# Waits of TensorE for its own last tile around the feed-forward loops, and other start addresses for the rows it reads

## The chip, the cores and the metric

The kernel runs on one core of one Trainium2 chip. The metric is the time of one execution on the device in microseconds (us); lower is better. Before the change three runs gave 2365.05, 2376.81 and 2380.16 us; their median is 2376.81 us.

## What is computed

Two small transformer-like stacks, one after the other, on 256 tokens of width 1024 in fp32 (the first stack adds 16 meta tokens in front, so it works on 272 columns, and drops them at its end). Cut to what matters here:

```python
# first stack: 2 layers, 272 tokens
h = concatenate([meta, x], axis=1)
for l in range(2):
    h = h + 0.5 * swiglu(rms_norm(h, ffn1_norm[l]), ffn1_w_gu[l], ffn1_w_down[l])
    u = rms_norm(h, mix_norm[l])
    c_q, c_kv, k_pe, hq, hf, hi, hg, ga, gb = split_cols(u @ w_in[l], IN_SPLITS)
    y_a = mla(...) @ w_proj_attn[l]          # latent attention
    y_b = hgrn2(...) @ w_proj_rec[l]         # gated recurrence
    h = h + (sigmoid(ga) * y_a + sigmoid(gb) * y_b) @ w_out[l]
    h = h + 0.5 * swiglu(rms_norm(h, ffn2_norm[l]), ffn2_w_gu[l], ffn2_w_down[l])
x = rms_norm(h, final_norm)[:, 16:]
# second stack: 2 layers, 256 tokens: macaron_ffn, mixer, macaron_ffn in each
#   swiglu_2(x, ...) = (silu(x @ w_gate) * (x @ w_up)) @ w_down, width 1024 -> 2816 -> 1024
#   mixer of layer 0: causal convolution and a linear recurrence; of layer 1: attention
```

There are eight feed-forwards (FFNs) of the same size in all: four in the first stack and four in the second. Since the meta columns are dropped at the end, the last FFN of the first stack already works on 256 columns only.

## The kernel before

**Numbers.** Activations lie in SBUF with the feature on the partition and the token on the column. Every fp32 matrix product is made of three matmuls of a 128x128 weight block: weights and inputs are both split into a high and a low part (`whi`, `wlo`; `x_..._hi`, `x_..._lo`), and TensorE adds wlo*xhi + whi*xlo + whi*xhi (`split_product`, L607, L608, L609; the same three in `first_tiles`, L667 to L669). The moving operand of each is one row of an input tile: 272 columns in the first stack, 256 in the second and in those parts of the first stack's last stages that no longer need the meta tokens.

**Weights.** SyncE streams weight chunks from HBM into a ring of four slots (`raw`). ScalarE rounds a chunk to `whi` (L1000), VectorE makes `wlo` as the difference (L1399) and counts it in the semaphore `lo_made`. TensorE waits for it before each output tile, and counts each finished tile in `tile_done`.

**An FFN** (`ffn` in the TensorE program): 44 output tiles of gate and up (24 matmuls each, numbered 0 to 43), then 8 output tiles of down (66 matmuls each). Tiles 0 to 7 are written out in code; tiles 8 to 43 are one hardware loop (`pe.Fori`, L711) of nine rounds of four tiles; down is another loop (L729) of four rounds of two tiles (in the second stack three rounds, the last one is written out). Among the early tiles TensorE also makes the column sums for the norm and broadcasts the result (`norm_back_drained`: the broadcast matmuls at L625, and then a wait for the semaphore of the last of them, `back_made`). F6, the FFN behind the keys and values, leaves that out, since its norm exists already.

**Addresses.** The input tiles of all stages share one place. Their bases are multiples of 256 bytes plus a shift: `SHIFT` = 64 for the stages `0` (first FFN of a layer, `x_first`), `1` (mixer, `x_mixer`) and all 256-column stages (`x_tokens`), `BACK_SHIFT` = 192 for stage `2` (`x_second`, the second FFN of layer 0). A row of the 272-column tiles is 320 columns, 1280 bytes long, so every row has the shift of its tile. The hidden tiles (`hid_first`, `hid_second`, `hid_tokens`) are laid out alike. `cut(t, k, c)` picks row k from column c on: c is 0, or 16 where the meta tokens are left out. In the mixer of layer 1 there are 19 tiles with c = 0 and 20 with c = 16, out of `x_mixer`: the latter start at 64 + 16*4 = 128 bytes from a multiple of 256. The tile `mid` (input of the mixer's last eight tiles) has rows of 1088 bytes from a multiple of 256, so its rows begin at 0, 64, 128 and 192 in turn.

**What sets the order.** Everything is written out by hand: each engine has its own program, and the semaphores tie them. The TensorE loop that is touched:

```python
with pe.Fori(2, FFN_GU_QUADS) as b:
    for k in range(RING):
        k8_tile(b + q, k, b * RING + j + k - 3, k, X[s], c)
```

`k8_tile` waits for `lo_made` (L654) and for the bank to be read (`tile_read`, L656), and then makes the 24 matmuls.

Of the kernel before, what the change touches and what calls it, by code (L numbers as in the profile page):

```python
# [19 lines left out]
T = SEQ + N_META  # L20
# [23 lines left out]
RING = 4  # L44
# [216 lines left out]
def program(nc, a):  # L261
    with ExitStack() as ctx:
# [17 lines left out]
        LINE, SHIFT, BACK_SHIFT, ROW = 256, 64, 192, T + 48  # L280
# [6 lines left out]
        def line_after(place):  # L287
# [4 lines left out]
        X = {0: pair_at("x_first", KD, xbase + SHIFT, ROW), 1: pair_at("x_mixer", KD, xbase + SHIFT, ROW),  # L292
             2: pair_at("x_second", KD, xbase + BACK_SHIFT, ROW), "last": x_tokens, "F4": x_tokens, "REC": x_tokens,
             "F5": x_tokens, "F6": x_tokens, "ATT": x_tokens, "F7": x_tokens}
        top[0] = xbase + BACK_SHIFT + 2 * KD * ROW * 4
# [22 lines left out]
        HID = {0: pair_at("hid_first", KF, hbase + SHIFT, ROW), 2: pair_at("hid_second", KF, hbase + BACK_SHIFT, ROW),  # L318
               "last": hid_tokens, "F4": hid_tokens, "F5": hid_tokens,
               "F6": hid_tokens, "F7": hid_tokens}  # L320
        hid_end, ebase = hbase + BACK_SHIFT + 2 * KF * ROW * 4, hbase + BACK_SHIFT + 2 * KF * SEQ * 4
# [150 lines left out]
        def layer_stage(l, which):  # L472
            q, j, n = ((0, 0, 0), (FFN_QUADS, FFN_TILES, 1), (FFN_QUADS + MIX_QUADS, FFN_TILES + MIX_TILES, 2))[which]
            return dict(q=l * LAYER_QUADS + q, j=l * LAYER_TILES + j, x=l * 3 + which, n=l * 3 + n,
                        f=l * 2 + which // 2, c=N_META if (l, which) == (DEPTH - 1, 2) else 0, layer=True, s="last" if (l, which) == (DEPTH - 1, 2) else which)
# [40 lines left out]
        AFTER = {0: 1, 2: 0, "last": "F4"}  # L516
# [82 lines left out]
        def _(pe):  # L599
# [86 lines left out]
            def inputs_ready(x):  # L686
                return lambda i: pe.wait_ge(x_lo_made, x * 8 + i + 1)
# [14 lines left out]
            def ffn(q, j, x, n, f, c, layer, s, main_norm=True):  # L702
# [8 lines left out]
                with pe.Fori(2, FFN_GU_QUADS) as b:  # L711
                    for k in range(RING):
                        k8_tile(b + q, k, b * RING + j + k - 3, k, X[s], c)
# [14 lines left out]

                with pe.Fori(0, FFN_DOWN_QUADS if layer else FFN_DOWN_QUADS - 1) as b:  # L729
                    down(b)  # L730
# [3 lines left out]
            def mixer(l):  # L734
# [4 lines left out]
                for step, i in MIXER:  # L739
                    if (step, i) == ("tile", 0):  # L740
                        first_tiles(q, 2, X[1], 0, inputs_ready(x), input_norm(x, n, 0))
                    elif step == "tile" and i > 1:
# [3 lines left out]
                        hi, lo, at_k = sources.get(TILE[t][0], (*X[1], 0))  # L746
# [1411 lines left out]
```

## Time and profile before

| | |
|---|---|
| median of 3 runs | 2376.81 us |
| the profiled execution's own time | 2368.04 us |
| its span, first to last instruction | 2366.3 us |
| TensorE matmuls, busy | 2246.4 us, 95% |
| TensorE weight loads | 2206.1 us, 93% |
| VectorE / ScalarE / GpSimd | 59% / 49% / 23% |
| mean granted TensorE clock | 0.976 |

How to read it: "busy" of TensorE is time in which at least one matmul is in the array. Matmuls overlap, so a row's "mean ns of one" is longer than the distance between two starts (here called the pitch), and in a stretch without a gap the pitch is the length of the stretch over the number of matmuls that start in it. A count of a window also takes in the two or so that only reach into it.

### The profile page before, as it was taken

What the parts mean: (1) busy time and instruction counts of PE and PEld (TensorE: products, weight loads), DVE (VectorE), ACT (ScalarE), POOL (GpSimd) and SP (SyncE); (2) the same over time, 40 slices, a digit from 0 to 9 for tenths busy, and PEclk for the clock granted to TensorE, in tenths of its full rate; (3) what the DMA queues carried; (4) which work ended last, traced back from release to release, by engine and by line L of the source; (5) the groups of instructions that cost most, each with busy time, mean ns of one, the idle gap of its engine ahead of it and who ended that gap; (6) DMA issues with size and microseconds to landing.
All of it is one profiled execution on the core that took longest, in us unless ns stands there. A gap on an engine that the chain in (4) does not pass through costs nothing.

```text
span 2366.3 us, 49110 instructions
## 1 busy us (share of the span) xinstructions
PE 2246.4 (95%) x18270; PEld 2206.1 (93%) x18270; DVE 1398.5 (59%) x1966; ACT 1161.2 (49%) x1752; POOL 555.6 (23%) x589
## 2 busy tenths in 40 slices
PE   7999999999999999999999999985999999978998
PEld 7999988999999999888999899985999999978998
DVE  6555866655555557756565555476664655465553
ACT  5444544454345436444454455466554545455553
POOL 4322000232213220001332242024431132111420
PEclk9999999999999999999999999997999999998999
DMA  6554423455546545233565466442565556532663
GB/s 210 186 188 154 149 90 117 141 170 171 184 142 195 187 157 166 87 98 117 161 199 192 141 197 200 156 161 89 179 211 169 195 179 199 176 114 87 200 203 116
DMA packets 99258, 380.47 MB, mean 161 GB/s; under 512 B 10911, under 2 KB 13087, under 8 KB 99016
## 3 DMA queue, kind: packets, MB, share of 16 engines
q1 hardware_dynamic: 99144, 378.91, 49.5%
q8 instruction: 76, 1.25, 0.2%
q14 instruction: 38, 0.31, 0.0%
HBM read 377.80 MB, written 3.16 MB: 161 GB/s over the span
## 4 chain that ended last, share of the span: by engine, by line
PE 86%; DVE 6%; ACT 3%; issue 2%; DVEq 1%; POOL 1%; DMA 0%; ACTq 0%; SPq 0%
PE bank L607 26%; PE bank L608 25%; PE bank L609 25%; ACT whi L1000 2%; PE bank L667 2%; DVE wlo L1399 2%; PE bank L668 2%; PE bank L669 2%; PE bank L884 1%; PE bank L625 1%; PE bank L794 1%; PE bank L873 0%; DVE cv L1735 0%; PE bank L863 0%; POOL outlo L2042 0%
## 5 line engine op out<-in xcount | busy, mean ns | idle before, releaser
L1399 DVE TENSOR_TENSOR wlo<-raw,whi 128x1024 fp32r<-128x1024 f32 (+1 forms) x660 | 869.6, 1329 | 528.2 <-ACT whi L1000 525.8
L1000 ACT ACTIVATE whi<-raw 128x1024 fp32r<-128x1024 f32 (+1 forms) x660 | 729.2, 1117 | 439.9 <-PE bank L609 401.9
L607 PE MATMUL bank<-x_tokens_hi,wlo 128*128 128x256 f32 x1784 | 498.7, 280 | 4.3 <-DVE z L1751 3.6
L608 PE MATMUL bank<-x_tokens_lo,whi 128*128 128x256 f32 x1784 | 497.1, 279 | 0.0
L609 PE MATMUL bank<-x_tokens_hi,whi 128*128 128x256 f32 x1784 | 497.1, 279 | 0.0
L607 PEld LDWEIGHTS bank<-x_tokens_hi,wlo 128*128 128x128 f32 x1784 | 338.9, 190 | 5.9 <-issue 3.8
L608 PEld LDWEIGHTS bank<-x_tokens_lo,whi 128*128 128x128 f32 x1784 | 336.3, 189 | 0.0
L609 PEld LDWEIGHTS bank<-x_tokens_hi,whi 128*128 128x128 f32 x1784 | 336.0, 188 | 0.0
L1980 POOL TENSOR_TENSOR z<-sil,z 128x256 f32<-128x256 f32 (+1 forms) x176 | 176.4, 1002 | 567.7 <-DVE z L1443 416.3
L609 PE MATMUL bank<-hid_tokens_hi,whi 128*128 128x256 f32 x880 | 244.7, 278 | 0.0
L607 PE MATMUL bank<-hid_tokens_hi,wlo 128*128 128x256 f32 x880 | 244.6, 278 | 0.0
L608 PE MATMUL bank<-hid_tokens_lo,whi 128*128 128x256 f32 x880 | 244.6, 278 | 0.0
L607 PE MATMUL bank<-x_first_hi,wlo 128*128 128x272 f32 x672 | 192.9, 287 | 0.1
L608 PE MATMUL bank<-x_first_lo,whi 128*128 128x272 f32 x672 | 192.5, 287 | 0.0
L609 PE MATMUL bank<-x_first_hi,whi 128*128 128x272 f32 x672 | 192.5, 287 | 0.0
L607 PE MATMUL bank<-x_mixer_hi,wlo 128*128 128x272 f32 (+1 forms) x592 | 177.4, 300 | 1.3 <-DVE sgb L1515 1.2
L608 PE MATMUL bank<-x_mixer_lo,whi 128*128 128x272 f32 (+1 forms) x592 | 172.7, 292 | 0.0
L609 PE MATMUL bank<-x_mixer_hi,whi 128*128 128x272 f32 (+1 forms) x592 | 172.4, 291 | 0.0
L607 PEld LDWEIGHTS bank<-hid_tokens_hi,wlo 128*128 128x128 f32 x880 | 166.7, 189 | 0.0
L608 PEld LDWEIGHTS bank<-hid_tokens_lo,whi 128*128 128x128 f32 x880 | 165.2, 188 | 0.0
L609 PEld LDWEIGHTS bank<-hid_tokens_hi,whi 128*128 128x128 f32 x880 | 165.2, 188 | 0.0
L607 PEld LDWEIGHTS bank<-x_first_hi,wlo 128*128 128x128 f32 x672 | 126.6, 188 | 0.5 <-PE bank L625 0.5
(378 smaller groups left out, 4958.7 us busy)
## 6 DMA issues: line engine op xcount, KB each, us to landing
raw<-ffn_gu SPq DMA_DIRECT2D x352, 512.0 KB, 3.7
raw<-ffn_down SPq DMA_DIRECT2D x128, 704.0 KB, 4.1
raw<-mix SPq DMA_DIRECT2D x120, 512.0 KB, 3.5
raw<-rec SPq DMA_DIRECT2D x28, 512.0 KB, 3.9
raw<-kv SPq DMA_DIRECT2D x16, 512.0 KB, 4.4
raw<-att SPq DMA_DIRECT2D x16, 512.0 KB, 3.9
bias_rows<-rows SPq DMA_DIRECT2D x8, 256.0 KB, 4.3
bias<-bias_rows SPq DMA_DIRECT2D x1, 1536.0 KB, 9.0
```

What stands on the lines that cost most here:

```text
L607: pe.matmul(out, wlo[:, slot, w], xh(i), start=(i == 0), stop=False)
L608: pe.matmul(out, whi[:, slot, w], xl(i), start=False, stop=False)
L609: mm = pe.matmul(out, whi[:, slot, w], xh(i), start=False, stop=(i == last))
L625: mm = pe.matmul(out[:, at_t + t:at_t + t + P], inv[:, at_col + i:at_col + i + 1].to_broadcast([P, P]), ident, start=True, stop=True)
L667: pe.matmul(out, wlo[:, k, w], cut(hi, i, c), start=(i == 0), stop=False)
L668: pe.matmul(out, whi[:, k, w], cut(lo, i, c), start=False, stop=False)
L669: return pe.matmul(out, whi[:, k, w], cut(hi, i, c), start=False, stop=(i == 7))
L794: mm = pe.matmul(bank[NORM][:, 3 * col + s:3 * col + s + 1], src[:, at_t:at_t + P], ones[:, 0:1], start=(k == 0), stop=(k == len(parts) - 1))
L884: return pe.matmul(bank[b][0:size_s, col:col + size_t], keys[:, hd, s:s + size_s], qd[:, hd, t:t + size_t], start=True, stop=True)
L1000: act.activation(whi[:, k, 0:cols], raw[:, k, 0:cols], ACT.Copy).then_inc(hi_made, 1)
L1399: dve.tensor_tensor(wlo[:, k, 0:cols], raw[:, k, 0:cols], whi[:, k, 0:cols].bitcast(F32), ALU.subtract).then_inc(lo_made, 1)
L1980: pool.tensor_tensor(z[:, 2 + p, c:T], sil[:, p, c:T], z[:, 2 + p, c:T], ALU.mult).then_inc(hid_made, 1)
```

## The change

In `ffn`, TensorE's program: the loop over gate and up is cut in two (rounds 2 and 3, then 4 to 10), and ahead of each of the two loops and of the loop of down stands a wait for the finish of TensorE's own last tile (`tile_done`). That makes three waits in each of eight FFNs. In the layout: `BACK_SHIFT` is gone; `x_second` and `hid_second` start at 64; the stages of layer 1 have tiles with names of their own, of which `x_late` and `hid_late` lie as `x_first` and `hid_first` did, and `x_late_mixer` starts at 0, so that its column 16 starts at 64. What lies behind the two areas moves up by 64 bytes.

```diff
@@ -277,7 +277,7 @@
-        LINE, SHIFT, BACK_SHIFT, ROW = 256, 64, 192, T + 48
+        LINE, SHIFT, ROW = 256, 64, T + 48
@@ -289,10 +289,11 @@
-        X = {0: pair_at("x_first", KD, xbase + SHIFT, ROW), 1: pair_at("x_mixer", KD, xbase + SHIFT, ROW),
-             2: pair_at("x_second", KD, xbase + BACK_SHIFT, ROW), "last": x_tokens, "F4": x_tokens, "REC": x_tokens,
-             "F5": x_tokens, "F6": x_tokens, "ATT": x_tokens, "F7": x_tokens}
-        top[0] = xbase + BACK_SHIFT + 2 * KD * ROW * 4
+        X = dict.fromkeys(("last", "F4", "REC", "F5", "F6", "ATT", "F7"), x_tokens)
+        X.update({0: pair_at("x_first", KD, xbase + 64, ROW), 1: pair_at("x_mixer", KD, xbase + 64, ROW),
+                  2: pair_at("x_second", KD, xbase + 64, ROW), "late": pair_at("x_late", KD, xbase + 64, ROW),
+                  "late_mixer": pair_at("x_late_mixer", KD, xbase, ROW)})
+        top[0] = xbase + LINE + 2 * KD * ROW * 4
@@ -315,10 +316,10 @@
-        HID = {0: pair_at("hid_first", KF, hbase + SHIFT, ROW), 2: pair_at("hid_second", KF, hbase + BACK_SHIFT, ROW),
...
+        HID.update({0: pair_at("hid_first", KF, hbase + 64, ROW), 2: pair_at("hid_second", KF, hbase + 64, ROW),
+                    "late": pair_at("hid_late", KF, hbase + 64, ROW)})
+        hid_end, ebase = hbase + LINE + 2 * KF * ROW * 4, hbase + LINE + 2 * KF * SEQ * 4
@@ -472,7 +473,8 @@
-                        f=l * 2 + which // 2, c=N_META if (l, which) == (DEPTH - 1, 2) else 0, layer=True, s="last" if (l, which) == (DEPTH - 1, 2) else which)
+                        f=l * 2 + which // 2, c=N_META if (l, which) == (DEPTH - 1, 2) else 0, layer=True,
+                        s=which if l < DEPTH - 1 else ("late", "late_mixer", "last")[which])
@@ -513,7 +515,7 @@
-        AFTER = {0: 1, 2: 0, "last": "F4"}
+        AFTER = {0: 1, 2: "late", "late": "late_mixer", "last": "F4"}
@@ -708,9 +710,11 @@
-                with pe.Fori(2, FFN_GU_QUADS) as b:
-                    for k in range(RING):
-                        k8_tile(b + q, k, b * RING + j + k - 3, k, X[s], c)
+                for first, end in ((2, 4), (4, FFN_GU_QUADS)):
+                    pe.wait_ge(tile_done, first * RING + j)
+                    with pe.Fori(first, end) as b:
+                        for k in range(RING):
+                            k8_tile(b + q, k, b * RING + j + k - 3, k, X[s], c)
@@ -726,6 +730,7 @@
+                pe.wait_ge(tile_done, j + 2 * KF)
                 with pe.Fori(0, FFN_DOWN_QUADS if layer else FFN_DOWN_QUADS - 1) as b:
                     down(b)
@@ -738,12 +743,12 @@
-                        first_tiles(q, 2, X[1], 0, inputs_ready(x), input_norm(x, n, 0))
+                        first_tiles(q, 2, X[st["s"]], 0, inputs_ready(x), input_norm(x, n, 0))
...
-                        hi, lo, at_k = sources.get(TILE[t][0], (*X[1], 0))
+                        hi, lo, at_k = sources.get(TILE[t][0], (*X[st["s"]], 0))
```

TensorE's instructions where the loop over gate and up begins, in the first FFN, before: the last three matmuls of tile 7, the jump into the loop and the loop's first tile. `bank` is the PSUM bank written.

```order
L607 MATMUL bank<-x_first_hi,wlo 128x272
L608 MATMUL bank<-x_first_lo,whi 128x272
L609 MATMUL bank<-x_first_hi,whi 128x272
L711 UNCONDITIONAL_BRANCH
L711 ISA
L656 REGISTER_ALU [waits lo_made]
L607 MATMUL bank<-x_first_hi,wlo 128x272 [waits tile_read]
```

The same place with the change. The jump now waits for `tile_done`, and the register instructions that set up the loop stand behind it.

```order
L609 MATMUL bank<-x_first_hi,wlo 128x272
L610 MATMUL bank<-x_first_lo,whi 128x272
L611 MATMUL bank<-x_first_hi,whi 128x272
L715 UNCONDITIONAL_BRANCH [waits tile_done]
L715 ISA
L658 REGISTER_ALU [waits lo_made]
L609 MATMUL bank<-x_first_hi,wlo 128x272 [waits tile_read]
```

TensorE where tile 15 ends and tile 16 begins, in the first FFN with the change: before, both are rounds of one loop, and here a second loop is entered.

```order
L609 MATMUL bank<-x_first_hi,wlo 128x272
L610 MATMUL bank<-x_first_lo,whi 128x272
L611 MATMUL bank<-x_first_hi,whi 128x272
L715 REGISTER_ALU
L715 COMPARE_AND_BRANCH
L715 UNCONDITIONAL_BRANCH [waits tile_done]
L715 ISA
L658 REGISTER_ALU [waits lo_made]
L609 MATMUL bank<-x_first_hi,wlo 128x272 [waits tile_read]
```

Moved or added are these jumps with their waits and set-up, and the second copy of the loop's body; TensorE's written program grows from 8854 to 9709 such rows. No other engine's program gets an instruction more or less.

## Rows read from the trace of the kernel before

**Rows 1.** Page: span, busy us (share) xinstructions, and the chain that ended last.
```profile
span 2366.3 us, 49110 instructions
PE 2246.4 (95%) x18270; PEld 2206.1 (93%) x18270; DVE 1398.5 (59%) x1966; ACT 1161.2 (49%) x1752; POOL 555.6 (23%) x589
PE 86%; DVE 6%; ACT 3%; issue 2%; DVEq 1%; POOL 1%; DMA 0%; ACTq 0%; SPq 0%
```

**Rows 2.** Windows, TensorE: stretch, length, busy (x matmuls), granted clock, DMA share, GB/s.
```profile
50.00:140.00 90.00, 90.00 (x732) 1.00 0.58 190
160.00:210.00 50.00, 50.00 (x407) 1.00 0.48 157
515.00:605.00 90.00, 90.00 (x713) 1.00 0.58 184
625.00:675.00 50.00, 50.00 (x397) 1.00 0.44 147
1190.00:1260.00 70.00, 70.00 (x596) 1.00 0.62 200
1280.00:1330.00 50.00, 50.00 (x427) 1.00 0.49 158
1385.00:1455.00 70.00, 70.00 (x620) 1.00 0.66 208
1470.00:1520.00 50.00, 50.00 (x443) 1.00 0.52 171
1695.00:1765.00 70.00, 70.00 (x620) 1.00 0.67 210
1920.00:2000.00 80.00, 80.00 (x682) 1.00 0.65 197
2215.00:2285.00 70.00, 70.00 (x620) 1.00 0.68 208
```

**Rows 3.** Timeline, TensorE, tile 10 of the first stack's last FFN: start, length.
```profile
1175.29 0.28 PE L609 MATMUL bank<-x_tokens_hi,whi 128*128 128x256 f32 x1
1175.40 0.31 PE L607 MATMUL bank<-x_tokens_hi,wlo 128*128 128x256 f32 x1
1175.55 0.28 PE L608 MATMUL bank<-x_tokens_lo,whi 128*128 128x256 f32 x1
```

**Rows 4.** Timeline, VectorE, same place: the low part that tile 10 waits for.
```profile
1173.98 1.22 DVE L1399 TENSOR_TENSOR wlo<-raw,whi 128x1024 fp32r<-128x1024 f32 x1 [3.35 <-ACT whi L1000]
```

**Rows 5.** Timeline, TensorE: a wait for its own last matmul, in that FFN.
```profile
1163.68 0.67 PE L625 MATMUL bank<-consts,inv 128*128 128x128 f32 x4
1164.41 0.38 PE L607 MATMUL bank<-x_tokens_hi,wlo 128*128 128x256 f32 x1
1164.63 0.28 PE L608 MATMUL bank<-x_tokens_lo,whi 128*128 128x256 f32 x1
1164.74 0.28 PE L609 MATMUL bank<-x_tokens_hi,whi 128*128 128x256 f32 x1
```

**Rows 6.** TensorE's sequencer at the loops' starts: min/median/max ns, first and last start.
```profile
L711 PEldq MOVE  x1: 29/29/29, 1167.9 to 1167.9; - x1
L656 PEldq FUSED_REGOPS  x1: 43/43/43, 1168.1 to 1168.1; - x1
L729 PEldq MOVE  x1: 29/29/29, 1269.7 to 1269.7; - x1
L719 PEldq EVENT_SEMAPHORE  x1: 51/51/51, 1270.1 to 1270.1; - x1
```

**Rows 7.** Groups by form, 925:931 (mixer, c = 16), then 465:480 (tile mid).
```profile
L607 PE MATMUL bank<-x_mixer_hi,wlo 128*128 128x256 f32 x18 | 5.1, 283 | 0.0
...
L608 PE MATMUL bank<-midlo,whi 128*128 128x272 f32 x41 | 11.8, 288 | 0.0
L607 PE MATMUL bank<-midhi,wlo 128*128 128x272 f32 x40 | 11.6, 290 | 0.0
```

**Rows 8.** Groups by form, 1388:1400 (F4, gate and up); below 1183:1200 (last FFN).
```profile
L608 PE MATMUL bank<-x_tokens_lo,whi 128*128 128x256 f32 x36 | 9.9, 276 | 0.0
...
L609 PE MATMUL bank<-x_tokens_hi,whi 128*128 128x256 f32 x49 | 13.8, 281 | 0.0
```

**Rows 9.** Page, DMA queues: packets, MB, share of 16 engines over the span.
```profile
q8 instruction: 76, 1.25, 0.2%
```

More of the change, by code:

```diff
@@ L317, in program @@
         hid_tokens = pair_at("hid_tokens", KF, hbase + SHIFT, SEQ)
-        HID = {0: pair_at("hid_first", KF, hbase + SHIFT, ROW), 2: pair_at("hid_second", KF, hbase + BACK_SHIFT, ROW),
-               "last": hid_tokens, "F4": hid_tokens, "F5": hid_tokens,
-               "F6": hid_tokens, "F7": hid_tokens}
-        hid_end, ebase = hbase + BACK_SHIFT + 2 * KF * ROW * 4, hbase + BACK_SHIFT + 2 * KF * SEQ * 4
+        HID = dict.fromkeys(("last", "F4", "F5", "F6", "F7"), hid_tokens)
+        HID.update({0: pair_at("hid_first", KF, hbase + 64, ROW), 2: pair_at("hid_second", KF, hbase + 64, ROW),
+                    "late": pair_at("hid_late", KF, hbase + 64, ROW)})
+        hid_end, ebase = hbase + LINE + 2 * KF * ROW * 4, hbase + LINE + 2 * KF * SEQ * 4
         H, E = [hbase], [ebase]
```

## Prediction

> **What bounds the kernel.** I read the page's busy shares and its chain first: TensorE has a matmul in the array for 95% of the span and holds 86% of the chain that ended last [rows 1]. So nearly every nanosecond on the distance between two matmul starts (the pitch) is in the time, and little else is. Next I asked for windows in the middle of the FFNs' loops, where TensorE is busy throughout, and divided length by matmuls (less two that only reach into the window) [rows 2]. The order of those rows is: first FFN's gate/up and down, second FFN's gate/up and down, the last FFN's of the first stack gate/up and down, F4's gate/up and down, then gate/up of F5, F6 and F7. The pitches come out as follows.
> - 272 columns, rows at 64: 90/730 = 123.3 ns and 50/405 = 123.5 ns. Rows at 192 (second FFN of layer 0): 90/711 = 126.6 ns and 50/395 = 126.6 ns.
> - 256 columns, all at 64: F4 70/618 = 113.3 and 50/441 = 113.4 ns, F5 and F7 the same 113.3; but the last FFN of the first stack 70/594 = 117.8 and 50/425 = 117.6 ns, and F6 80/680 = 117.6 ns.
>
> The second line is the interesting one: one loop body, one layout, one granted clock (1.00), and two pitches. The timeline shows where the last FFN leaves the faster one: at tile 10 a matmul's successor comes 0.15 us later instead of 0.113, and behind it the steps are 0.12 [rows 3]. That tile waits for its low weights, which VectorE finishes at 1173.98 + 1.22 = 1175.20 us, after 3.35 us without work of its own [rows 4]; TensorE's queue had nearly run dry. I take it that how weight loads and matmuls interleave in the queue is a pattern that lasts until something disturbs it: a near-stall can leave the longer pitch, and a full stop brings the shorter one back, since after the stop at the norm's broadcast the pitch of that FFN is 0.11 us [rows 5], up to tile 10.
>
> **The waits, their gain.** If each loop starts from an empty array, the last FFN keeps 113.3 ns for tiles 10 to 43 and for down: 34*24*4.5 ns = 3.7 us and 8*66*4.3 ns = 2.3 us. F6, which has no such stop before, gains 36*24*4.3 ns = 3.7 us in its loop and, with the last FFN's price for down, 2.3 us. Together 12.0 us. At 272 columns I take nothing: pitch is 123.3 ns at 64 in all windows read, although those FFNs have the stop at the broadcast too, so no shorter pitch shows. F4, F5 and F7 have 113.3 ns already. The near-stall at tile 10 should not come back: the weights' chain runs on while TensorE stands 0.6 us at tile 8, so tile 10 is wanted 0.6 us later.
>
> **The waits, their cost.** There are 3*8 = 24. The nearest row is the stop at the broadcast: the four broadcast matmuls end at 1163.68 + 0.67 = 1164.35, so the last began at about 1164.07; two matmuls on is 1164.63, that is 0.56 us for two steps of 0.113: 0.33 us lost [rows 5]. Here more hangs behind the wait: the sequencer's set-up of the loop, which before ran ahead hidden by the queue. From the set-up's first instruction to its last before a matmul I read 1167.9 to 1168.1 us, some 0.25 us with the last one's length and the wake-up, for gate and up, and 1269.7 to 1270.1, some 0.45 us, for down [rows 6]. So 16*(0.33 + 0.25) + 8*(0.33 + 0.45) = 9.3 + 6.2 = 15.5 us. Lower bound: set-up hidden, 24*0.33 = 7.9 us. Upper bound: each start also pays one code chunk. The code queue moved 76 packets in 0.2% of 16 engines' span [rows 9], 0.002*16*2366/76 = 1.0 us each: 15.5 + 24 = 39.5 us. I take 15.5, since the taken jumps back in these loops leave no gap in windows that are busy throughout [rows 2]. Behind each wait only TensorE's own next tile is queued. VectorE and ScalarE get slack from it; the weight stream's slots come free 0.6 us later at a time, which nobody waits for while TensorE is the bound.
>
> The Trainium skill ("TensorE: Matmul & The Clock Gate", single matmul latency and back-to-back issue gap) gives (398+N)/2.4 ns for one warm matmul and N/2.4 + 2.5 ns between two, at N = 256 272.5 and 109.2 ns: a stop would cost 163 ns, an estimate from that page, and 24 of them 3.9 us; the trace's 0.33 us disagrees and decides.
>
> **Second FFN's rows at 64.** 44*24 matmuls at 126.6 - 123.3 = 3.3 ns: 3.5 us; 8*66 at 3.1 ns: 1.7 us. The two patterns do not blur this, as both FFNs have a stop at the broadcast and both keep their pitch. Gain 5.2 us; bounds 0 (the address isn't the cause) and 5.2.
>
> **Late mixer.** No row shows 272 columns from 0 alone. Tile `mid` has rows at 0, 64, 128, 192 in turn, and its matmuls take 288 to 290 ns [rows 7]. A matmul's length is its pitch and 163 ns more (276 at 113.3, 281 at 117.8) [rows 8, 2], so that is 126 ns on average, and rows at 0 and 128 would be at (4*126 - 123.3 - 126.6)/2 = 127.0 ns. The 19 tiles with c = 0 then lose 456*3.7 ns = 1.7 us (bounds 0 and 2.1). The 20 tiles with c = 16 go from 283 - 163 = 120 ns [rows 7] to 117.7 or 113.3, whichever pattern they are in: 480*2.3 = 1.1 or 480*6.7 = 3.2 us; I take the middle, 2.1. Net gain 0.4 us, between -1.0 and +3.2. The shift by 64 bytes of what lies behind the tiles is costed at nothing: those are operands of engines off the chain.
>
> **Sum.** Against the profiled execution's own 2368.0 us: -12.0 - 5.2 - 0.4 + 15.5 = -2.1, so 2366 us. That execution is 8.8 us below the runs' median. The runs span 15.1 us; if executions differ in how many FFNs run at 117.7 ns (6.0 us each), the median had one or two more than the profile, and the change would take those away too. I can't see that from one trace; I leave the forecast at 2366 and let the range reach up by most of those 8.8 us and more.
>
> **Rivals.**
> - *The short pitch is not kept* (0.12): another near-stall, or the new loop's first round, throws the FFNs back. For: F6 and the last FFN stayed at 117.7 ns for 100 us each. Against: F4, F5, F7 stay at 113.3 through their first round. Then the 12.0 us stay away: 2378 us.
> - *Slower, by code fetch behind the stops* (0.06): the program grows by 855 written rows, and an empty queue covers no fetch. At one chunk per stop 2366 + 24 = 2390 us; it decides for "slower" from (2400.6 - 2366)/24 = 1.4 us more per stop, 2 us in all, which is about two chunks (0.03). The Trainium skill ("Runtime: NRT & Kernel Launch", instruction fetch mechanics) says that a taken branch whose target isn't in the current two-page window forces a fetch before execution goes on; the loops' jumps back show no such gap here.
> - *The stops are cheap* (0.12): set-up hidden, 7.9 us, and the mixer's better end: 2368 - 12.0 - 5.2 - 3.2 + 7.9 = 2355.5 us, and further down only if other FFNs gain as well.
> - *Addresses do nothing* (0.05): 126.6 against 123.3 ns has another cause: 2366 + 5.6 = 2371.5 us. By the skill's gap formula, which knows no address, 272 columns take 115.8 ns anywhere; the rows at 64 and at 192 differ, so I trust it little here.
> - The forecast has the remaining 0.65.
>
> **Numbers.** A measurement of this kernel can tell about 1% from no change: 2353.0 to 2400.6 us. The forecast and three rivals lie inside; faster takes the far end of the cheap stops (0.05), slower two chunks at each stop (0.03), the rest 0.92. The range is 2354 to 2381: from the cheap stops to the short pitch not kept, with some of the runs' own spread.
>
> **What would show it.** TensorE's windows in the last FFN and F6 at 113.3 ns and in the second FFN at 123.3 ns show the gains right. Twenty-four new holes of 0.6 (gate/up) and 0.8 us (down) show the cost right; 0.33 or 1.6 us make the number wrong by 7 or 24 us. In the late mixer the matmuls with 272 columns should last 290 ns instead of 286, those with 256 between 276 and 281 instead of 283. A near-stall in rounds 2 and 3 that outlives the second stop would make the first term wrong.

## The result and the profile after

The changed kernel took 2388.95 us (median of 9 runs, 2383.79 to 2393.91) against 2372.30 us before (9 runs, 2365.05 to 2386.32): a ratio of 1.0065, 95% interval 1.0041 to 1.0088. It is slower by about 0.65%. That is inside the 1% called "the same" above, but it is a real loss, on the other side of the forecast's sign, and outside its range. The profiled execution took 2384.87 us, against 2368.04 before: 16.8 us more, which is what the medians differ by too.

The page of the changed kernel, against [rows 1] and [rows 9]. TensorE has the same 18270 matmuls, and is busy 5.8 us longer; the span is 16.8 us longer.

```profile
span 2383.1 us, 49118 instructions
PE 2252.2 (95%) x18270; PEld 2206.2 (93%) x18270; DVE 1402.8 (59%) x1966; ACT 1163.2 (49%) x1752; POOL 549.2 (23%) x589
q8 instruction: 82, 1.34, 0.2%
PE 82%; DVE 6%; ACT 5%; issue 3%; DVEq 2%; POOL 1%; POOLq 1%; DMA 0%; ACTq 0%; SPq 0%
```

Windows of TensorE in the changed kernel, 60 us in tiles 16 to 43 and 45 us in down, columns as in [rows 2]. In this order: second FFN of layer 0; last FFN; F4; F5; F6; F7.

```profile
541.00:601.00 60.00, 60.00 (x489) 1.00 0.59 176
625.00:670.00 45.00, 45.00 (x367) 1.00 0.47 155
1201.00:1261.00 60.00, 60.00 (x532) 1.00 0.64 201
1278.00:1323.00 45.00, 45.00 (x384) 1.00 0.49 161
1396.00:1456.00 60.00, 60.00 (x532) 1.00 0.64 202
1473.00:1518.00 45.00, 45.00 (x384) 1.00 0.48 162
1711.00:1771.00 60.00, 60.00 (x531) 1.00 0.64 203
1788.00:1833.00 45.00, 45.00 (x385) 1.00 0.48 159
1952.00:2012.00 60.00, 60.00 (x532) 1.00 0.63 198
2029.00:2074.00 45.00, 45.00 (x384) 1.00 0.49 164
2238.00:2298.00 60.00, 60.00 (x532) 1.00 0.64 201
2315.00:2360.00 45.00, 45.00 (x384) 1.00 0.42 136
```

Take two off each count, as in the prediction. The second FFN stands at 60/487 = 123.2 and 45/365 = 123.3 ns where it was 126.6: as forecast. Gate and up stand at 60/530 = 113.2 ns in all five FFNs with 256 columns: also as forecast. But down stands at 45/382 = 117.8 ns in **all five**, also in F4, which ran it at 113.4 before [rows 2].

The stop ahead of down in F4, from TensorE's timeline of the changed kernel (start, length, instruction): the last matmul of tile 43, then the first three of down.

```profile
1467.20 0.28 PE L611 MATMUL bank<-x_tokens_hi,whi 128*128 128x256 f32 x1
1468.03 0.35 PE L609 MATMUL bank<-hid_tokens_hi,wlo 128*128 128x256 f32 x1 [0.55 <-DVE wlo L1404]
1468.22 0.28 PE L610 MATMUL bank<-hid_tokens_lo,whi 128*128 128x256 f32 x1
1468.34 0.28 PE L611 MATMUL bank<-hid_tokens_hi,whi 128*128 128x256 f32 x1
```

And the first stop of F4, between tiles 7 and 8:

```profile
1368.03 0.28 PE L611 MATMUL bank<-x_tokens_hi,whi 128*128 128x256 f32 x1
1368.65 0.38 PE L609 MATMUL bank<-x_tokens_hi,wlo 128*128 128x256 f32 x1 [0.35 <-DVE z L1441]
1368.87 0.28 PE L610 MATMUL bank<-x_tokens_lo,whi 128*128 128x256 f32 x1
1368.99 0.28 PE L611 MATMUL bank<-x_tokens_hi,whi 128*128 128x256 f32 x1
```

The releasers named in brackets had long been done; what the wait is for is TensorE's own tile, and the profile puts it down to another semaphore. At down 0.83 us pass to the next start and then 0.19, for two steps of 0.113: 0.79 us lost. At the first stop it is 0.62 and 0.22, so 0.61 us lost. The forecast had 0.78 and 0.58.

The loops' entries, TensorE's sequencer: 16 set-ups for gate and up and 8 for down, where the profile of before has 8 and 8.

```profile
L715 PEldq MOVE  x16: 29/29/34, 44.8 to 2232.6; - x16
L734 PEldq MOVE  x8: 29/29/34, 152.5 to 2309.4; - x8
```

In the late mixer (groups by form, 928:934, then 898:922) the matmuls with 256 columns last 276 ns where they lasted 283 [rows 7], and those with 272 columns last 290, that is a pitch of 127.

```profile
L609 PE MATMUL bank<-x_late_mixer_hi,wlo 128*128 128x256 f32 x19 | 5.2, 276 | 0.0
...
L610 PE MATMUL bank<-x_late_mixer_lo,whi 128*128 128x272 f32 x64 | 18.5, 290 | 0.0
```

Two stretches outside the FFNs grew that no edit touches: the mixer's sums of layer 1, and the attention's scores and probabilities with the matmuls around them. The first window runs from the first matmul of the sums to the first broadcast matmul behind the tile that follows them; the second takes the same 112 matmuls in both kernels, the last two dozen of them already in the tiles behind the attention. Before:

```profile
1007.40:1019.40 12.00, 12.00 (x81) 0.72 0.17 53
2109.40:2147.00 37.60, 22.99 (x112) 0.86 0.09 29
```

After:

```profile
1009.87:1023.50 13.63, 13.63 (x81) 0.62 0.14 44
2117.80:2159.20 41.40, 27.61 (x113) 0.71 0.08 27
```

The mean granted clock was lower there: 0.62 against 0.72, and 0.71 against 0.86, so that more of the stretch ran at 1.2 GHz and less at 2.4.

### The profile page after: what moved, and what is told of

The parts are those of the page before. It is cut to its first block, busy times and chain, and to the rows that moved or that the text cites. A ratio compares the mean times of both kernels' runs of the same rounds, so it can differ in the third digit from the quotient of the medians.

```text
span 2383.1 us, 49118 instructions
## 1 busy us (share of the span) xinstructions
PE 2252.2 (95%) x18270; PEld 2206.2 (93%) x18270; DVE 1402.8 (59%) x1966; ACT 1163.2 (49%) x1752; POOL 549.2 (23%) x589
## 4 chain that ended last, share of the span: by engine, by line
PE 82%; DVE 6%; ACT 5%; issue 3%; DVEq 2%; POOL 1%; POOLq 1%; DMA 0%; ACTq 0%; SPq 0%
PE bank L609 24%; PE bank L610 24%; PE bank L611 24%; ACT whi L1005 3%; DVE wlo L1404 2%; PE bank L669 1%; PE bank L670 1%; PE bank L671 1%; PE bank L889 1%; PE bank L627 1%; PE bank L799 1%; POOLq L1965 1%; PE bank L878 0%; DVE cv L1740 0%; PE bank L868 0%
## 5 line engine op out<-in xcount | busy, mean ns | idle before, releaser
L1985 POOL TENSOR_TENSOR z<-sil,z 128x256 f32<-128x256 f32 (+1 forms) x176 | 167.1, 949 | 573.3 <-DVE z L1448 424.5
L1441 DVE TENSOR_TENSOR z<-bank,rstd 128x256 f32<-128x256 f32 (+1 forms) x176 | 75.4, 428 | 74.6 <-PE bank L611 61.4
L1989 POOL TENSOR_TENSOR hid_tokens_lo<-z,hid_tokens_hi 128x256 f32 x110 | 100.1, 910 | 79.6 <-ACT hid_tokens_hi L1072 79.6
L1448 DVE TENSOR_TENSOR z<-bank,rstd 128x256 f32<-128x256 f32 (+1 forms) x176 | 75.2, 427 | 55.7 <-PE bank L611 48.5
L609 PE MATMUL bank<-x_second_hi,wlo 128*128 128x272 f32 x336 | 96.7, 288 | 0.8 <-DVE wlo L1404 0.4
L609 PE MATMUL bank<-x_late_hi,wlo 128*128 128x272 f32 x336 | 96.7, 288 | 0.8 <-DVE wlo L1404 0.4
L609 PE MATMUL bank<-x_first_hi,wlo 128*128 128x272 f32 x336 | 96.7, 288 | 0.7 <-DVE wlo L1404 0.3
L610 PE MATMUL bank<-x_second_lo,whi 128*128 128x272 f32 x336 | 96.3, 287 | 0.0
```

The lines of the kernel that those rows point to most:

```text
L609: pe.matmul(out, wlo[:, slot, w], xh(i), start=(i == 0), stop=False)
L610: pe.matmul(out, whi[:, slot, w], xl(i), start=False, stop=False)
L1441: dve.tensor_tensor(z[:, p, c:T], bank[banks[2 * p]][:, 0:T - c], rstd[:, c:T], ALU.mult).then_inc(tile_read, 1)
L1448: dve.tensor_tensor(z[:, 2 + p, c:T], bank[banks[2 * p + 1]][:, 0:T - c], rstd[:, c:T], ALU.mult).then_inc(tile_read, 1)
L1985: pool.tensor_tensor(z[:, 2 + p, c:T], sil[:, p, c:T], z[:, 2 + p, c:T], ALU.mult).then_inc(hid_made, 1)
L1989: pool.tensor_tensor(cut(HID[s][1], at_i, c), z[:, 2 + p:3 + p, c:T], cut(HID[s][0], at_i, c).bitcast(F32), ALU.subtract).then_inc(hid_lo_ ...
```

## The ledger

Cut at the first matmul of each stage, the two profiled executions compare so (us, minus is a gain):

| term of the prediction | forecast | in the two profiles |
|---|---|---|
| 24 stops | +15.5 | +16.1 |
| gate and up, last FFN and F6 | -7.4 | -7.5 |
| down, last FFN and F6 | -4.6 | 0 |
| down, F4, F5 and F7 | 0 | +7.0 |
| second FFN's rows at 64 | -5.2 | -5.2 |
| late mixer | -0.4 | +0.8 |
| mixer of layer 0; attention; recurrence and keys/values; early tiles | 0 | +1.9; +3.7; +0.8; -0.8 |
| sum | -2.1 | +16.8 |

The stops' 16.1 is the length by which the first FFN of layer 1 grew (2.01 us, with nothing else changed in it) times eight; 16 * 0.61 + 8 * 0.79 gives 16.1 too. Down is 62.19 us at 117.8 ns and 59.85 at 113.3, from its first matmul to the one behind it; a long one costs 2.3 us. Of the miss of 18.9 us, 11.6 are in down alone.

## Experiments

Where a theory is named, the first is mine: the waits cost their stops, and the pitch behind them decides what they give back. In the tables "L" is the long pitch (117.8 ns) and "s" the short one (113.3), first letter tiles 16 to 43, second letter down, in the order last FFN, F4, F5, F6, F7. A ratio is always to the kernel before on the same chip.

**Each part alone.** First the addresses without the waits (one loop again), and the changed kernel without the wait ahead of down.

```diff
-                for first, end in ((2, 4), (4, FFN_GU_QUADS)):
-                    pe.wait_ge(tile_done, first * RING + j)
-                    with pe.Fori(first, end) as b:
+                with pe.Fori(2, FFN_GU_QUADS) as b:
...
-                pe.wait_ge(tile_done, j + 2 * KF)
```

> The kernel before with the new addresses alone: no new wait, one loop. Theory A (the addresses act only through the matmuls that read these rows): the second FFN of layer 0 goes from 202.3 to about 197.3 us, the late mixer changes by -1 to +1 us, the first mixer and the stage ATT stay at 265.6 and 88.7 us; about 5 us less than before, 2367 us. Theory B (the move of everything behind by 64 bytes costs time: in the changed kernel the first mixer took 1.9 us and ATT 3.7 us more): mixer 267.5 and ATT 92.4 us here too, and the gain is used up: 2372 us.

Measured: 2363.80 us, ratio 0.9982 (0.9949 to 1.0014), near theory A. The second FFN of layer 0 went from 202.3 to 197.1 us, -5.2, as forecast; the late mixer from 264.9 to 263.25, -1.65. So the addresses do what was said. The profile's span is still 2374.5 us, 8 above that of before: its pattern is LL LL LL ss LL, two FFNs more at the long pitch, which is 10.6 us.

The changed kernel with both loops and both their waits, less the one wait ahead of down:

```diff
-                pe.wait_ge(tile_done, j + 2 * KF)
```

> The changed kernel without the wait ahead of down; the two waits of gate and up stay. Theory A (the stop ahead of down is what puts down at 117.7 ns a matmul in the 256-column FFNs; without it down goes on at the pitch of gate and up): down of F4, F5, F6, F7 and of the first stack's last FFN takes about 59.9 us instead of 62.3 to 64.6 (the last one 62.1 with its norm), 5 x 2.4 = 12 us, and 8 stops of 0.75 us go, 6 us: about 18 us less than the changed kernel, 2371 us. Theory B (the hidden tiles' new places or the split loop give 117.7 ns): down stays at 62.3 us, only the 6 us go: 2383 us.

Measured: 2385.08 us, ratio 1.0034 (1.0000 to 1.0069). Pattern LL LL LL LL ss. The time is near theory B's 2383 us, but down had the pitch of its gate and up in all five, as theory A says; only that pitch was the long one. Here gate and up ran at the long pitch behind two stops each in four FFNs of five, in the same code that ran it short five times in the profile after. That alone broke the step "a full stop brings the shorter pitch back".

**The stop at down placed later.** The first round of down is written out, and the wait stands directly ahead of its first matmul, so that the set-up is done before TensorE stands still.

```diff
+                        if isinstance(b, int) and b == 0 and m == 0:
+                            pe.wait_ge(tile_done, j + 2 * KF)
...
-                pe.wait_ge(tile_done, j + 2 * KF)
-                with pe.Fori(0, FFN_DOWN_QUADS if layer else FFN_DOWN_QUADS - 1) as b:
+                down(0)
+                with pe.Fori(1, FFN_DOWN_QUADS if layer else FFN_DOWN_QUADS - 1) as b:
```

> The changed kernel with the first round of down written out ahead of its loop, and the wait for tile_done moved to directly ahead of down's first matmul, behind all set-up and the other waits. Theory A1 (the pitch after a stop depends on how the first weight load and matmul follow the sequencer's last instructions; with the stop last, as at the norm's broadcast, it can settle at 113.3 ns): down takes 59.9 us in the 256-column FFNs, and each stop there costs 0.35 instead of 0.75 us: 12 + 3 us less than the changed kernel, 2374 us. Theory A2 (any full stop ahead of the hidden rows ends at 117.7 ns): down stays at 62.3 us, only 3 us go: 2386 us.

Measured: 2380.35 us, ratio 1.0053 (1.0027 to 1.0078). The stop fell from 0.82 to 0.43 us between starts, so the sequencer's set-up is some 0.4 us, near the 0.45 that the prediction gave it. The pitch behind it was still long in all five: sL sL sL sL sL, theory A2.

**The same kernels profiled again: the one before, the changed one, the one without the wait ahead of down.**

> The kernel before once more, for its profile. Theory A (the pitch pattern belongs to the program): the first stack's last FFN and F6 at 117.7 ns, F4, F5, F7 at 113.3 ns again. Theory B (it differs between executions): other FFNs at 117.7 ns, each 6 us; this would be the spread of 2365 to 2386 us in the runs of before.

Measured: 2386.16 us, span 2384.3, for the kernel before, unedited. Its windows in the last FFN (gate/up, down) and in F7:

```profile
1201.00:1261.00 60.00, 60.00 (x512) 1.00 0.63 195
1280.00:1325.00 45.00, 45.00 (x385) 1.00 0.48 166
2242.00:2302.00 60.00, 60.00 (x532) 1.00 0.67 208
2318.00:2363.00 45.00, 45.00 (x399) 1.00 0.43 144
```

The pattern is LL LL LL LL ss where the profile that the prediction was made from has LL ss ss LL ss: two FFNs more at the long pitch, 2 * 5.3 = 10.6 us of the 18. So one profile of the kernel before doesn't tell its pattern: theory B.

> The changed kernel once more, for its profile. Theory A (each stop ahead of down ends at 117.7 ns because of how that stop ends: first weight load 31 ns ahead of its matmul, second matmul 193 ns on; 10 of 10 so far in two profiles): down at 62.3 us in all five 256-column FFNs again. Theory C (every stop draws one of the two pitches anew, by something that differs between executions, and down only had bad draws): some of the five downs at 59.9 us.

Measured: 2381.87 us; again sL sL sL sL sL, as theory A has it. A third profile, below, takes that back.

> The changed kernel without the wait ahead of down once more, for its profile. Theory C (a stop draws the pitch anew, differently from execution to execution): the ten loops of gate and up in 256-column FFNs, of which one execution had 8 at 117.8 ns and the changed kernel 1 of 10, come out in another pattern. Theory A (the program decides): the same 8 again.

Measured: 2366.43 us, on the same chip as its first profile at 2390.98 us. The windows of the last FFN, in that first profile, then here:

```profile
1199.00:1259.00 60.00, 60.00 (x512) 1.00 0.64 193
1278.00:1323.00 45.00, 45.00 (x385) 1.00 0.52 167
```

```profile
1200.00:1260.00 60.00, 60.00 (x532) 1.00 0.67 202
1276.00:1321.00 45.00, 45.00 (x399) 1.00 0.51 166
```

One program, one chip, and LL LL LL LL ss against ss ss ss ss ss: 4 * (2.97 + 2.34) = 21.2 of the 24.6 us between the two executions. The program alone doesn't decide the pitch.

**A small delay behind the stop.** Three waits that are fulfilled already stand ahead of the fourth matmul of the first tile of each round of down.

```diff
+                            if i == 1 and m == 0:
+                                pe.wait_ge(lo_made, (b + q + FFN_GU_QUADS) * RING + 1)
+                                pe.wait_ge(tile_read, b * 2 + j + 2 * KF - 1)
+                                pe.wait_ge(hid_lo_made, f * KF + KF - 2)
```

> The changed kernel with three waits that are long fulfilled ahead of the fourth matmul of the first tile of each round of down: right behind the stop the sequencer falls some 0.1 to 0.3 us behind there. In the traces a stop that ends at 113.3 ns always has one step of 122 to 124 ns or a slow run-out of 119, 116, 114 among its first four, and one that ends at 117.7 has none. Theory D (such a small delay is what brings the short pitch): down takes about 60 us instead of 62.3 in the five 256-column FFNs, 12 us less than the changed kernel, 2377 us. Theory A (the stop ahead of down ends at 117.7 whatever follows): 62.3 us stays, 2389 us.

Measured: 2383.13 us, ratio 1.0065 (1.0044 to 1.0086); LL ss ss ss ss. The time lies between the two theories, and it looked like a way to the short pitch, four downs of five. The second profile below took that away.

**No stop at all in an FFN.** The addresses are the new ones, the waits are out as in the first diff, and the wait of the norm's broadcast for its own matmul is out too.

```diff
-                        norm_back_drained(n, c)
+                        norm_back(n, c)
```

> The new addresses alone (no new wait), and in the FFNs the wait behind the norm's broadcast is taken away too, so no stop is left in an FFN; the stages between them keep theirs. Theory C (a stop only draws anew): each FFN goes through at the pitch it starts with, mostly the one its stage began with, and its five stops of 0.33 us and three of the 272-column FFNs go, 2.6 us; the time spreads as that of the kernel with the addresses alone, about 2362 us. Rival (the stop at the broadcast gives the short pitch more often than not): the five FFNs stay at 117.7 ns, 5 x 6 us, up to 15 us more than the addresses alone, 2375 us.

Measured: 2358.27 us, ratio 0.9960 (0.9932 to 0.9987), span 2354.0, pattern ss ss ss LL ss: near theory C's 2362 us. Four FFNs ran short without a single stop written into them. The same kernel, timed again in more rounds on another chip:

> The new addresses without any stop in an FFN (no new wait, and the old one behind the norm's broadcast taken out) once more, with more rounds: it was 0.996 times before. The theory that a stop costs its 0.33 to 0.8 us and brings the short pitch no more surely than going on does expects the same again, 0.994 to 0.998, and FFNs at 113.3 ns in part; a rival (its draws of pitch were lucky in that execution's chip) expects about 0.998, that of the addresses alone.

Measured: 2368.58 us, ratio 1.0001 (0.9976 to 1.0026), span 2374.8, pattern ss LL LL LL LL. The gain did not come again, and both theories had forecast some; the two intervals hardly touch. The pattern is a likely reason (three FFNs more at the long pitch, 16 us, between the two profiles), but one profile of each doesn't show it for the other runs.

**Only the wait ahead of down; and the three waits at the old addresses.** The first is the changed kernel with one loop again, the second the kernel before with the waits and the cut loop of the change's diff.

> The new addresses and of the three waits only the one ahead of down; gate and up are one loop without a wait. Theory A (that stop puts down at 117.7 ns whatever went before; 15 of 15 so far, all of them behind gate and up with stops at 113.3): down at 62.2 to 62.3 us in all five 256-column FFNs, and the 8 stops cost 0.75 us each: against the addresses alone 6 us for the stops and 2.3 us for each down that would have been at 113.3, some 6 to 14 us more, 2370 to 2378 us with before at 2368. Theory E (the pitch behind that stop depends on the pitch ahead of it): where gate and up ran at 117.8 ns, down comes out at 113.3 ns (59.9 us).

Measured: 2369.30 us, ratio 1.0002 (0.9971 to 1.0033); ss ss LL LL ss. Neither theory holds: three downs are short, against A, and the two behind a long gate and up are long, against E. Eight stops of 0.79 us are 6.3 us, 0.27%; with the addresses' -0.18% that makes +0.09%.

> The kernel before with the three waits and the split loop alone, at the old addresses: the other half of the change. If the two halves add up, it is slower than the whole change by what the addresses give: the second FFN of layer 0 at 126.6 ns instead of 123.3 (5.1 us) and the late mixer (0 to 2 us), so 1.009 to 1.010 times before, 2389 to 2392 us with before at 2368. If the addresses have a part in the pitch behind the stops (another theory of why down went to 117.7 ns), the downs come out at 59.9 us here.

Measured: 2390.96 us, ratio 1.0098 (1.0069 to 1.0128); Ls LL LL Ls Ls. The waits alone cost about 1%, more than the whole change, as forecast. Three of the five downs are short here, but the changed kernel has that too in its third profile below, so it doesn't speak for the addresses.

**Does the program or the execution decide?** Four more profiles of kernels that had been profiled already.

> The changed kernel, unedited, looked at a third time. Open is what decides the pitch behind the stop ahead of down: in the first two profiles of this kernel all ten downs at 256 columns ran at 117.8 ns (62.3 us each). Theory A, the program decides: five more at 117.8 ns, span 2380 to 2384 us. Theory B, the execution decides, all feed-forwards of one execution alike: another pattern is possible, down at 113.3 ns in all five (59.9 us each, 11.6 us less in all) or gate and up at 117.8 ns (79.9 instead of 77.0 us for tiles 16 to 43).

Measured: 2392.07 us. The changed kernel, in the windows of the last FFN, F4 and F5:

```profile
1200.00:1260.00 60.00, 60.00 (x511) 1.00 0.64 194
1280.00:1325.00 45.00, 45.00 (x399) 1.00 0.49 159
1398.00:1458.00 60.00, 60.00 (x511) 1.00 0.64 191
1478.00:1523.00 45.00, 45.00 (x385) 1.00 0.47 158
1716.00:1776.00 60.00, 60.00 (x512) 1.00 0.62 190
1796.00:1841.00 45.00, 45.00 (x399) 1.00 0.51 163
```

Gate and up are now long in all five FFNs, and down is short in three: Ls LL Ls Ls LL. Theory B, and neither letter is the program's. This profile was on another chip than the second one, so for this kernel the chip isn't excluded; for the kernel without the down wait it is. The stop ahead of down in F5, with the short pitch behind it, beside the one of F4 shown above:

```profile
1790.21 0.28 PE L611 MATMUL bank<-x_tokens_hi,whi 128*128 128x256 f32 x1
1791.06 0.36 PE L609 MATMUL bank<-hid_tokens_hi,wlo 128*128 128x256 f32 x1 [0.58 <-DVE wlo L1404]
1791.25 0.28 PE L610 MATMUL bank<-hid_tokens_lo,whi 128*128 128x256 f32 x1
```

0.85 and 0.19 us here, 0.83 and 0.19 there: the two differ by a few hundredths of a microsecond, and each matmul of down behind them by 4.5 ns. (They differ in one thing more: ahead of this stop the pitch is the long one, ahead of F4's it was the short one.)

> The changed kernel with three already fulfilled waits ahead of the fourth matmul of each down round's first tile, looked at again. Its first profile had down at 113.3 ns in four feed-forwards of five. Theory A, the program decides (the small delay behind the stop brings the short pitch): four or five of five at 113.3 ns again, 59.9 us each. Theory B, the execution decides: the count may be anything, all or none the likeliest.

Measured: 2397.24 us; ss LL ss LL LL. Two downs of five short, not four: the fulfilled waits don't bring the short pitch. Theory B. Down did have the pitch of its gate and up in ten cases of ten over the two profiles, where the changed kernel has that in two of fifteen. But the delay is not needed for a short down: the six short downs show steps of 0.195, 0.116 and 0.114 us ahead of the fourth matmul already, and so do three downs without the delay (two in the kernel with only the wait ahead of down, one in the second profile of the kernel with the waits at the old addresses). Down in the second FFN of layer 0, at 64 and with 272 columns:

```profile
624.00:669.00 45.00, 45.00 (x357) 1.00 0.46 153
```

45/355 = 126.8 ns, where [rows 2] has 123.5 at 64. So 272 columns have a longer pitch at 64 as well. It shows up only behind a stop ahead of down, in 6 of 25 such downs, and costs 1.75 us each time; without that stop all 21 stand at 123.3. Two more are in these profiles at 192, and both stand at 126.8, which the address alone gives.

> The kernel before with the three waits and the cut loop, at the old addresses, looked at again. Its first profile had tiles 16 to 43 at 117.8 ns in all five feed-forwards with 256 columns (79.9 us each), and down at 113.3 in three of five. Theory A: the same again, span 2398 us. Theory B: another pattern, with tiles 16 to 43 at 113.3 ns the span is up to 15 us less, 2383 us.

Measured: 2396.65 us; ss LL Ls Ls LL. Theory B: the time is near that of the first profile, the pattern is another.

> The kernel before, unedited, looked at a third time. It had gate and up at 117.8 ns in two of the five feed-forwards with 256 columns in one profile (span 2366.3 us) and in four of five in the other (2384.3 us). Theory A: two of five, and the 18 us came from elsewhere. Theory B: any count, with about 6 us of span for each feed-forward whose gate, up and down run at 117.8 ns.

Measured: 2368.87 us; LL ss ss ss LL. Two FFNs long as in the first profile of before, but F7 instead of F6: theory B, in the pattern and not in the count.

## Counts over all profiles

Seventeen profiles, five FFNs with 256 columns in each:

| | long pitch |
|---|---|
| tiles 16 to 43, no wait ahead (7 profiles) | 19 of 35 |
| tiles 16 to 43, waits ahead (10 profiles) | 22 of 50 |
| down, no wait ahead (8 profiles) | 21 of 40, always the pitch of the tiles before it |
| down, wait ahead (9 profiles) | 27 of 45, with the pitch before it or against it |

A stop cuts the inheritance: down without its own wait had the pitch of its gate and up in 40 cases of 40, and with it in 22 of 45. On the whole it doesn't choose: 54% long without and 44% with the waits in gate and up, 53% and 60% in down. The cases of one execution aren't independent either: in six of the ten profiles with waits gate and up are all long or all short. In us, a long gate and up (tiles 16 to 43) costs 3.0 (79.15 against 76.16) and a long down 2.3. The three profiles of before average 14.2 us of this, the three of the changed kernel 14.3. So the waits gave nothing back on average: they cost 16.1 us, 0.68%. With the addresses' -0.18% that is +0.50%, inside the interval of the measured +0.65% (0.41 to 0.88). The spans say the same: 2372.6 us on average over three profiles of before and 2384.5 over three of the changed kernel, 11.9 us or 0.50% more. Of these 11.9 us the terms in this document give 9.4 (16.1 for the stops, -5.2 and -1.65 for the addresses, 0.1 for the pitches); the rest is open. The waits alone, at the old addresses, measured somewhat more than 0.68% (0.69 to 1.28). Their two profiles have 18.0 us of long pitch on average, 3.9 more than before, and a long down at 272 columns in each, and with these the sum is 0.92%.

No version here is surely faster than the kernel before. The one without any stop lay beyond its interval once (0.9932 to 0.9987), and its repetition in more rounds didn't bear that out (1.0001, 0.9976 to 1.0026). The layout alone is the part worth keeping: 5.2 us in the second FFN, seen in every profile without a wait ahead of down, though a ratio of 0.9982 (0.9949 to 1.0014) can't show it against a pattern that moves 20 us.

## Why the prediction was wrong, point by point

- **TensorE's pitch is what counts**: right for the FFNs and the late mixer's tiles; by the ledger the stops, the pitches and the late mixer make 11.2 of the 16.8 us. The other 5.6 us are the last point of this list.
- **The cost of the stops**: right, 16.1 for 15.5 us; 0.61 and 0.79 us for 0.58 and 0.78. The set-up of the loop is part of it: taking it out (the wait directly ahead of the matmul) shortened down's stop from 0.82 to 0.43 us. The estimate of 163 ns from the Trainium skill ("TensorE: Matmul & The Clock Gate", single matmul latency and back-to-back issue gap) was far too low for this; the trace had decided rightly. That section gives its gap for isolated matmuls and says that in a stream of weight loads and matmuls both set the spacing, so the 115.8 ns that the prediction took from it for 272 columns was no figure for this stream either.
- **Second FFN's rows at 64**: right, -5.2 us in the layout alone; in the profile after its stage is 3.2 us shorter, with 2.0 us of its own three stops in that. The rival "addresses do nothing" is out. What I did not see is that 272 columns have two pitches as well, in down behind a stop.
- **"A full stop brings the shorter one back"**: this is the step that failed. I read it off one place, the stop at the norm's broadcast in the last FFN [rows 5], and off F4, F5 and F7 at 113.3 ns [rows 2]. But the pitch was the short one ahead of that stop too, 0.11 us, so nothing was brought back there:

```profile
1163.34 0.28 PE L607 MATMUL bank<-x_tokens_hi,wlo 128*128 128x256 f32 x1
1163.45 0.28 PE L608 MATMUL bank<-x_tokens_lo,whi 128*128 128x256 f32 x1
1163.57 0.28 PE L609 MATMUL bank<-x_tokens_hi,whi 128*128 128x256 f32 x1
```

  In the profile of after that same stop was followed by the long pitch:

```profile
1166.59 0.61 PE L627 MATMUL bank<-consts,inv 128*128 128x128 f32 x4
1167.25 0.38 PE L609 MATMUL bank<-x_tokens_hi,wlo 128*128 128x256 f32 x1
1167.47 0.28 PE L610 MATMUL bank<-x_tokens_lo,whi 128*128 128x256 f32 x1
1167.59 0.28 PE L611 MATMUL bank<-x_tokens_hi,whi 128*128 128x256 f32 x1
1167.71 0.28 PE L609 MATMUL bank<-x_tokens_hi,wlo 128*128 128x256 f32 x1
```

  The steps behind it are 0.12 here, 0.11 in [rows 5]. A stop draws the pitch anew and may as well take the short one away, as it did in F4, F5 and F7 (+7.0 us). The prediction priced only the gain: its rival "the short pitch is not kept" goes back to what was, 2378 us, and no case had FFNs that run short before and long after. With that case, down long everywhere, the sum is -2.1 + 4.6 + 7.0 = +9.5, so 2377.5 us, and gate and up long too would add the 7.4 us counted as gained and 3.0 us in each of F4, F5 and F7, 16.4 us more: 2394. The two sides of a draw belonged in the range.
- **The near-stall at tile 10**: right, it did not come back. In the seven profiles without waits in gate and up TensorE comes to tile 10 at the short pitch in 24 of 35 FFNs; each time one step at that tile is 0.14 to 0.36 us long, and in 8 of them the pitch is the long one from there on. In the 50 FFNs with the waits no step behind the stop in tiles 8 to 15 is longer than 0.12 us. So the waits take away what lengthened the pitch before, and their own stops lengthen it about as often.
- **The median and the pattern**: the text asked whether executions differ in how many FFNs run long, and took it that the change would mend that too. They do differ (two, four and two of five in three profiles of before); the change doesn't mend it.
- **Late mixer**: the pitches came as put down where they were read, 127 ns from 0 (126.6 start to start) and 113.3 for column 16 (length 276 ns); some later tiles from column 16 run at 117.8. By the layout alone the mixer gained 1.65 us, within the bounds; in the profile after it lost 0.8, with 1.65 us from the sums at the lower clock.
- **Code fetch behind the stops** (2390 us): the time came close to this rival's, the mechanism did not. The code queue moved 82 packets for 76 [rows 9], and no stop is a code chunk's 1.0 us longer than another: TensorE's stops ahead of gate and up lie between 0.62 and 0.65 us in the last FFN, F4, F5, F6 and F7 alike, and those ahead of down between 0.82 and 0.87 in all eight. The Trainium skill ("Runtime: NRT & Kernel Launch", instruction fetch mechanics) speaks of a fetch when a branch leaves the window; the loops' entries show none here.
- **What else moved**: 5.6 us outside the FFNs that I costed at nothing. The sums in the mixer take 11.8 to 12.2 or 13.5 to 13.8 us, in either layer, in profiles of the same kernel (of before: 12.0, 13.6 and 12.0 in layer 1), and the attention's stretch 37.6, 40.2 and 39.4 us in the three profiles of before (41.4 in the profile after). So these differ between executions of one kernel, and the profile after had both sums and the attention at their long end. Whether the waits make the lower clock likelier isn't settled: the sums of layer 0 were long in 7 of 10 profiles with waits in gate and up, and in 2 of 7 without.

## What stays open

What decides which pitch follows a stop is not settled. It isn't the written order (same kernel, both pitches), nor the stop's kind (0.33, 0.43, 0.62 and 0.82 us were each followed by the long pitch somewhere), nor a short delay behind it. The interval between starts at the stop seems to go with it: down's stops of 825 ns were followed by the long pitch 11 times in 11, those of 827 ns by the short one 3 times in 3, gate and up's of 619 ns by the long one 13 times in 13, those of 617 ns by the short one 9 times in 9; but 616, 621 and 822 ns had both. The pitch ahead may have a part in it as well: behind the stop between tiles 15 and 16 the pitch was the same as ahead of it in 35 cases of 50, but behind the one ahead of down only in 22 of 45. These are readings after the fact; no run set such an offset on purpose. The runs' times hint at one thing that the waits may do: 8 to 10 runs of a kernel with waits in gate and up lie within 6 to 15 us, and those without within 20 to 40 us (9 to 27 runs). But the second profile of the kernel without the down wait, 2366.43 us, lies 10.5 us below the lowest of its first ten runs, so the narrow spread isn't shown to hold.

## What to carry to other kernels

If one loop body shows two pitches in one profile, take several profiles of the unchanged kernel before you explain them: the pattern may belong to the execution. A mechanism that restores a good state must be priced with the places that are in that state already, since it can take them out of it. A wait of TensorE for its own last matmul costs 0.33 to 0.39 us by itself here, 0.61 with the set-up of the loop over gate and up behind it and 0.79 with that of down; against a gain of 4.5 ns a matmul the last two need 135 to 175 matmuls that surely become shorter to pay.

## What the runs showed of the hardware

- TensorE runs the same stream of weight loads and matmuls at one of two lasting pitches, 113.3 or 117.8 ns at 256 columns and 123.3 or 126.8 ns at 272, at a granted clock of 1.00, for up to 141 us on end (tiles 16 to 43 and down of the last FFN before); where the pitch changed in the places read, a stop or a near-stall stood ahead.
- The start address of the rows is in the pitch: 272 columns take 123.3 ns at 64 (126.8 in 6 downs behind a stop), 126.6 at 0 and 126.7 at 192; 256 columns take 113.3 or 117.8 at 64 and 120 at 128.
- One kernel on one chip gave 2366.43 and 2390.98 us with nothing changed, and 21.2 us of that are four FFNs at the other pitch.
- The sums' stretch of layer 1 took 12.00 us at a mean granted clock of 0.72 and 13.63 us at 0.62; both lengths occur in profiles of one kernel.
